# Widening the column blocks of a dense value product on one Trainium2 core: three blocks of 384 become 512, 512 and 128

## The reference, cut to what matters

```
idx = ...                                  # (T, 8, 16), expert numbers of each token
h = gelu(einsum('thkd,td->thk', U[idx], x))
w = gate * h
y = einsum('thk,thkd->td', w, V[idx])      # V: 16384 x 2048
h = h + y
```

## Time and profile before

| | before |
|---|---|
| runs | 3560.3, 3562.12, 3566.16 us; median 3562.12 |
| profiled execution | 3560.3 us, its span 3558.6 us |
| mean granted TensorE clock | 0.995 of full speed |
| TensorE passes, busy | 3496.7 us, 98% of the span |
| TensorE weight loads, busy | 3182.4 us, 89% |
| VectorE | 2144.4 us, 60% |
| GpSimd | 1048.1 us, 29% |
| ScalarE | 635.5 us, 18% |
| line 1553, passes of 128x384 | 1536, from 1948.1 to about 2472 us |

### The profile page before, as it was taken

The page is one execution under the profiler, slowest core; times in us unless marked ns, Lnnn a source line. Parts: engine busy times, 40 slices in busy tenths (PEclk is TensorE's granted clock), DMA queues, the critical chain, the costliest instruction groups (busy, mean ns, idle before and its releaser), DMA issues. The chain is left out here.

```text
span 3558.6 us, 51078 instructions
## 1 busy us (share of the span) xinstructions
PE 3496.7 (98%) x20690; PEld 3182.4 (89%) x20690; DVE 2144.4 (60%) x4178; ACT 635.5 (18%) x1425; POOL 1048.1 (29%) x797
## 2 busy tenths in 40 slices
PE   8999999999999999999999999999999999999999
PEld 7878887899998888888888899998999999999988
DVE  4884102145555499966798766665366766766653
ACT  0002202100001212222366200001222122222100
POOL 0000100010000055575596788784000121122000
PEclk9999999999999999999999999999999999999999
DMA  6434432244454589999997799998334322222452
GB/s 223 142 130 142 142 130 96 106 163 172 172 221 185 231 299 401 403 409 409 340 343 276 283 408 406 408 406 322 122 142 154 119 97 89 94 101 72 157 202 103
DMA packets 159591, 785.05 MB, mean 221 GB/s; under 512 B 19540, under 2 KB 21484, under 8 KB 123644
## 3 DMA queue, kind: packets, MB, share of 16 engines
q1 hardware_dynamic: 101112, 510.14, 38.3%
q0 software_dynamic: 57344, 268.47, 19.5%
q10 hardware_dynamic: 900, 3.17, 0.3%
HBM read 771.06 MB, written 10.64 MB: 220 GB/s over the span
## 5 line engine op out<-in xcount | busy, mean ns | idle before, releaser
L424 PE MATMUL PS<-mem,ring 128*128 128x272 f32 (+1 forms) x2816 | 646.7, 392 | 1.2 <-DVE mem L938 1.2
L424 PEld LDWEIGHTS PS<-mem,ring 128*128 128x128 f32 x2816 | 540.9, 193 | 105.4 <-issue 6.8
L1334 POOL DMA_INDIRECT mem<-in_peer_ug,idx x256 | 359.8, 1405 | 530.2 <-DVE idx L1949 335.3
L1363 POOL DMA_INDIRECT mem<-in_peer_vg,idx x256 | 378.4, 1478 | 107.0 <-issue 81.5
L2086 DVE SCALAR_TENSOR_TENSOR mem<-mem 128x896 f32<-128x896 f32 x256 | 294.8, 1152 | 175.3 <-DMA mem<-in_peer_vg,idx 174.4
L2002 DVE CUSTOM_DVE_ANT_0 mem<-mem 128x1152 f32<-128x1152 f32 x256 | 348.7, 1363 | 81.9 <-DMA mem<-in_peer_ug,idx 78.6
L1475 PE MATMUL PS<-mem 128*128 128x256 f32 x1792 | 387.5, 379 | 1.3 <-DMA mem<-in_peer_ud 1.3
L1475 PEld LDWEIGHTS PS<-mem 128*128 128x128 f32 x1792 | 340.2, 190 | 48.2 <-DMA mem<-in_peer_ud 2.1
L432 PEld LDWEIGHTS PS<-mem,ring 128*128 128x128 f32 x3136 | 350.3, 192 | 0.1
L432 PE MATMUL PS<-mem,ring 128*128 128x128 f32 x3136 | 350.3, 275 | 0.0
L2385 POOL TENSOR_TENSOR mem<-mem,ring 128x512 f32<-128x512 f32 x84 | 114.7, 1381 | 693.6 <-DVE mem L3128 512.9
(11 more groups left out here) (439 smaller groups left out, 4466.3 us busy)
## 6 DMA issues: line engine op xcount, KB each, us to landing
ring<-in_first_tiles SPq DMA_DIRECT2D x143, 1024.0 KB, 4.8
ring<-in_dn_tiles SPq DMA_DIRECT2D x88, 1024.0 KB, 5.0
mem<-in_peer_vd SPq DMA_DIRECT2D x128, 576.0 KB, 8.1
mem<-in_peer_ud SPq DMA_DIRECT2D x128, 448.0 KB
ring<-in_out_panels SPq DMA_DIRECT2D x16, 2048.0 KB, 9.2
ring<-in_w_out SPq DMA_DIRECT2D x8, 2048.0 KB, 11.8
ring<-in_peer_wq SPq DMA_DIRECT2D x8, 2048.0 KB, 9.6
mem<-second_keys SPq DMA_DIRECT2D x64, 256.0 KB
```

The costliest lines, as they stand in the source:

```text
L424: last = nc.tensor.matmul(PS[:, 4 + n % 4, 0:T if wide else TX], wslots[slot_of[n]][:, k, :], x, start=(k == 0), stop=(k == KT - 1))
L1334: nc.gpsimd.indirect_dma_start(ugs[at % US], None, a["peer_ug"], bass.IndirectOffsetOnAxis(ap=idx[:, n, j:j + 1], axis=0)).then_inc(u_in[a ...
L1363: nc.gpsimd.indirect_dma_start(vgs[at % GS], None, a["peer_vg"], bass.IndirectOffsetOnAxis(ap=idx[:, n, j:j + 1], axis=0)).then_inc(vg_in[ ...
```

## The change

The block width is no longer 384 but the width of a PSUM bank, 512. A group of 1152 columns is cut as 512 + 512 + 128: the two full blocks fill banks `2m` and `2m + 1`, the last takes 128 columns of bank `4 + m`. The number of matmuls stays three for each key and token half. `add_dense` follows: one addition of 1024 columns, read from the two banks as one row of neighbours, and one of 128.

```diff
-CD, VW = 1152, 384
+CD = 1152
...
-                        for at in range(0, CD, VW):
-                            to = PS[:, 2 * m + at // VW if at < 2 * VW else 4 + m, 0:VW]
-                            last = nc.tensor.matmul(to, weights_of[m][:, i // LO, :, i % LO], vds[i % VS][:, at:at + VW],
+                        for at in range(0, CD, BANK):
+                            w = min(BANK, CD - at)
+                            to = PS[:, 2 * m + at // BANK, :] if w == BANK else PS[:, 4 + m, 0:w]
+                            last = nc.tensor.matmul(to, weights_of[m][:, i // LO, :, i % LO], vds[i % VS][:, at:at + w],
                                                     start=(i == 0), stop=(i == NKEY - 1))
...
-                        hc = h_tok[:, m, 0:2 * VW].rearrange("p (b n) -> p b n", n=VW)
-                        nc.vector.tensor_tensor(hc, hc, PS[:, 2 * m:2 * m + 2, 0:VW], ALU.add).then_inc(y_added, 1)
-                        hc = h_tok[:, m, 2 * VW:CD]
-                        nc.vector.tensor_tensor(hc, hc, PS[:, 4 + m, 0:VW], ALU.add).then_inc(y_added, 1)
+                        hc = h_tok[:, m, 0:2 * BANK]
+                        nc.vector.tensor_tensor(hc, hc, PS[:, 2 * m:2 * m + 2, :].rearrange("p b n -> p (b n)"),
+                                                ALU.add).then_inc(y_added, 1)
+                        hc, w = h_tok[:, m, 2 * BANK:CD], CD - 2 * BANK
+                        nc.vector.tensor_tensor(hc, hc, PS[:, 4 + m, 0:w], ALU.add).then_inc(y_added, 1)
                         dve.wait_ge(y_added, 2 * m + 2)
```

## The result

| | before | after |
|---|---|---|
| median of the runs | 3561.97 us (4 runs) | 3616.64 us (4 runs) |
| profiled execution's span | 3558.6 us | 3613.2 us |
| ratio | | 1.0156, 95% interval 1.0139 to 1.0174 |

What follows compares the result with a forecast made beforehand. TensorE was taken to bound the kernel, busy 98% of the span. Terms 56.2 + 0.3 - 1.2 - 0.1 = +55 us on the median of 3562.1 gave 3617 us, +1.5%; range of 8 in 10: 3604 to 3630.

Steps and rivals of the forecast that it cites:

- What bounds the stage: Line 1553's stage: TensorE sets the pace, busy 490.32 of 491.40 us; the DMA engines, 99% busy, are just fast enough.
- Rival C: Line 1553's stage belongs to the DMA engines, so slower TensorE eats into waits: +28 us, 3590 us; chance 4%.
- 512 columns at 429.2 ns: Pitch of a 512-column pass, taken from another stage; four such passes in each new group of line 1553.
- Which loads are hidden: Line 1553's spread weight loads are hidden whole under passes of 384 or 512 columns, but not under 128 columns.
- Rival A: Line 1553's loads are hidden anyway, fetched while a 512-column pass runs; group stays at 1940 ns, 3560 to 3564 us; 6%.
- 220 ns for the short pass: Each of a group's two 128-column passes costs 220 ns with a spread load behind it, read behind line 1542's one-hot products.
- Rival B: Behind a short pass of line 1553 a spread load costs its whole 295 ns record: +94 us, 3656 us; chance 7%.
- Stalls of the loads: Two holes before line 1553 from loads of `vds`, 1.5 us in all, can go: -1.2 us taken.
- The sum: 253 groups of line 1553 give +56.2 us; other groups +0.3, stalls -1.2, last pass -0.1: +55 us.
- The adds: Accumulator adds at lines 2035 and 2037: 1.22 + 0.28 = 1.50 us, the same as before.

Runs made afterwards that it cites:

- packed kernels: Kernel before (384-column blocks) and changed kernel (512 + 512 + 128), each with LO = 1, a key's weights next to each other: 3602.26 and 3603.70 us.
- packed_384: Kernel before, three blocks of 384, with LO = 1 so that a key's 128 weights are neighbours: 3602.26 us, ratio 1.0114.
- load_step1: Changed kernel with the stationary operand read as 128 neighbouring elements instead of 16 apart, values not the reference's: 3561.66 us, ratio 1.0002.
- third_256: Kernel before with blocks of 448 + 448 + 256 instead of three of 384, weights still 16 apart: 3564.49 us, ratio 1.0013.
- step 2: Changed kernel with stationary elements 2 apart instead of 16, values not the reference's: 3565.58 us, ratio 1.0015.
- step 3: Changed kernel with stationary elements 3 apart instead of 16, values not the reference's: 3597.15 us, one execution.
- step 4: Changed kernel with stationary elements 4 apart instead of 16, values not the reference's: 3623.82 us, ratio 1.0183.
- Steps 4 and 8: Changed kernel with stationary elements 4 or 8 apart instead of 16, values not the reference's: 3623.82 us and, in one execution, 3624.36 us.
- 5 and 16: Changed kernel with stationary elements 5 apart, values not the reference's: 3618.78 us, one execution; 16 apart is the changed kernel itself, 3616.64 us.

## Why the prediction was right

- **What bounds the stage.** Right. What a group costs more, 2.150 - 1.935 = 0.215 us where I had added 0.222, came through as time. Rival C, the DMA engines as the true limit, would have shown holes; there are none, and the DMA share fell to 91%.
- **512 columns at 429.2 ns.** Right: the packed kernels' group of 1.94 us is 4 x 429.2 + 2 x 112.
- **Which loads are hidden.** Right, and shown from both sides: short loads take the cost away at the new widths, and long loads cost nothing under passes of 384 columns (the kernel before has loads of 295 ns, packed_384 of 190, and both have groups of 1.935 us). Rival A, loads fetched further ahead, would have left the change at 3560 to 3564 us.
- **220 ns for the short pass.** Slightly high. Two spread loads in a row behave like the single one behind the one-hot products: 217 ns. That is 2 x 3.4 ns x 253 = 1.7 us of the sum. Rival B, the whole record of 295 ns, fell with the measured group, and again with the 256-column block.
- **Stalls of the loads.** They went altogether, and were worth a little more than the 1.5 us that I had read. By the starts of the groups around them, (2016.43 - 2011.52) - 2 x 1.935 = 1.04 and (2291.99 - 2287.33) - 2 x 1.935 = 0.79: 1.8 us, of which my sum took 1.2.
- **The sum, place by place.** These are TensorE's passes behind the stage, first before, then after:

```profile
2471.94 3.73 PE L1598 MATMUL PS<-mem 128*128 128x128 f32 x32
...
2483.32 7.09 PE L2496 MATMUL PS<-mem 128*56 128x256 f32 x32 [2.34 <-PEq L119]
```

```profile
2524.87 3.74 PE L1599 MATMUL PS<-mem 128*128 128x128 f32 x32
...
2536.25 8.77 PE L2498 MATMUL PS<-mem 128*56 128x256 f32 x32 [2.33 <-PEq L119]
```

The shift up to line 1598 (1599) is 2524.87 - 2471.94 = 52.9 us. Its parts are +0.5 us up to the start of the stage (1980.93 against 1980.46), 253 x 0.215 = +54.4 for the groups, -1.8 for the stalls, and -0.1 because the first group of the stage stood behind a short pass before too. My sum said 55.2: 1.7 too much for the short pass, 0.6 too little for the stalls that went.
- **The rest of the difference is luck.** The spans differ by 54.6 us, so 1.7 us more came later. They are in the two rows above: the same 32 passes took 7.09 us before and 8.77 after. Between 2536.20 and 2539.60 us the granted clock was 0.52 of full speed after, the lower of TensorE's two levels (1.2 GHz) nearly throughout, and 1.00 before in the same place; ahead of it TensorE had been idle for 2.3 us in both. The change does not bring this with it: the trace of load_step1, which has its widths, shows 7.08 us there, and that of third_256, which costs next to nothing in the stage, 8.77. My sum was 2.3 us too high for what the change does, and a stretch at the lower clock made most of it up in the profiled execution. That the medians met the forecast to half a microsecond is no measure of the sum.
- **The adds.** 1.22 + 0.28 us measured, 1.22 + 0.28 forecast.

No version tried beats the kernel before. A group must stream 1152 columns twice; by the pitches of this case three blocks of 384 do that in 1.935 us, as little as any cut here, and hide every load.

## What to carry to other kernels

Each pass must be wide enough to hide the load of the *next* stationary operand; a remainder block pays for the load and not for its columns, so cut a width into equal blocks rather than into full banks and a rest. Price the load by its layout first: look for passes of the same layout behind a short pass anywhere in the trace, as one place of six passes gave this change's whole cost within 3%. A record's length is neither the price of a pass nor of a load. Starts are, if they are taken over a whole group: the wait for a late load shows at the pass behind it, here as 0.38 us on a short pass and 0.70 us on a wide one, although both waits come from short passes that hide too little.

## What the runs showed of the hardware that I had not expected

- An fp32 weight load of 128 elements that is not hidden has a price of 112 ns or less packed, 117 at step 2, 174 at step 3, and 217 to 237 from step 4 on. Steps 4 and 8 are a little dearer (232, 237 ns) than 5 and 16 (219, 217). Why 16 is cheaper than 8 was not looked into.
- The moving operand pays for a spread read too: line 1499's passes of 128 columns went from 280 to 395 ns of record, and from 0.11 to 0.22 us from start to start, when its elements lay 128 apart and not in runs of 16.
- A late load stretches the record of the pass that waits for it (593 to 620 ns on the mean for 512 columns) and appears nowhere as idle time: TensorE was "busy" for 543.87 of 543.90 us while 253 x 0.21 = 53 us of that, a tenth, was waiting for weights.
